# Block 1's query and index stages: a third pair of buffers, merged copies, small PSUM banks, pooled rows kept apart

## The chip, the cores and the metric

The kernel runs on one core of a Trainium2 chip. A core has five engines that run their own instruction streams and meet at semaphores: TensorE (PE, matrix products into PSUM), ScalarE (ACT), VectorE (DVE), GpSimd (POOL) and SyncE (SP, which here only issues DMAs). The metric is the device time of one execution in microseconds, as the median of several runs.

## The reference, cut to what matters

The program is two transformer blocks, one after the other, over 1024 tokens of width 1024 in float32. Only block 1 is touched. It has two layers over T = 1040 tokens (16 meta tokens and 1024 rows of x), and each layer does this:

```
proj = rms_norm(x) @ w_in            # q, k, v, gate_a, u_b, gate_b, q_idx, k_idx, w_idx, merge
q = rope(rms_norm(q per head)); k = rope(rms_norm(k)); q_idx = rope(q_idx); k_idx = rope(k_idx)
score = sum_h relu(q_idx[h] . k_idx) * w_idx[h]     # 8 index heads
attn  = softmax attention of 8 heads over the 256 best-scored visible keys of each query
y_a   = (attn * silu(gate_a)) @ w_a
pooled = windowed mean of u_b (windows 2, 4, 8, 16) minus u_b
y_b   = ((pooled @ pool_w + pool_b) * pool_s * silu(gate_b)) @ w_b
x     = x + (sigmoid(merge_a) * y_a + sigmoid(merge_b) * y_b) @ w_out
```

## The kernel before, in words

Everything is held transposed: features lie on the 128 partitions and tokens (1040, padded to TP = 1044) along the free dimension. A projection of 128 output features is a "job". `project` (L683 and around it) waits for its weights, claims a PSUM area and issues 8 chunks x 3 products x 3 pieces of 348 columns, 72 matmuls, all of them at L689. The three products per chunk come from splitting each float32 operand into a high and a low part of a faster float type. Two engines prepare the weights of every job: ACT makes the high part (`weight_hi`, L1263), POOL the low part (`weight_lo`, a subtraction at L1832). Both do so two jobs ahead, in the call `after(job)`: after a job is emptied, the weights of the job two further on are split.

The order on each engine is written out by hand, one program per engine, and semaphores join them. An engine that waits holds back all that stands behind it in its own program. PSUM: `big[0]` and `big[1]` have three banks each and are claimed in turn by `claim`, which first waits until the last user of that area has been emptied; `small2` (two banks, halves `small[0]` and `small[1]`) is free during the query stage.

The query stage of a layer treats four pairs of heads (chunks c = 0 to 3), then the index key `ki` with the 8 index weights, then key and value `kv`, then the first index query `qi`. For chunk c:

- PE projects q(c). ACT takes it out of PSUM twice (L1461 the square, L1462 the copy with the gain) into the pair of buffers `sc4[2*(c%2)]` and `sc4[2*(c%2)+1]`, then splits weights (`after`).
- PE makes the mean of the squares (`head_square`) and the rotated copy (`rotated`), both by `plain` (L701).
- DVE adds epsilon (`variance`, L2169), which also empties the `head_square` area. ACT does the reciprocal root in three steps with two table loads (`root`, L1376 to L1380).
- POOL multiplies by the cosine (`times_cos`, L1859). DVE multiplies the rotated copy by the sine (L2180), adds (L2457), finishes the root (L2173, L2174) and multiplies (L2461): the chunk is `roped`.
- ACT writes the high parts of the two heads into QS (`split_q`, L1446, two instructions). DVE subtracts to get the low parts (`stack_q`, L2188, two instructions, `q_stacked`). Only after them comes DVE's `variance` of the next chunk.

On PE the order is project q(c), `head_square` and `rotated` of chunk c-1, project q(c+1). On ACT it is, for each c: take q(c) out, `root` of c-1, `split_q` of c-1. Because chunk c+2 uses the buffers of chunk c, taking it out waits for `q_stacked` of chunk c.

The index stage (`index_stage`, L1008 scores, L999 rotations) has four chunks of 14 score units. PE alternates between `big[1]` and `small2` for the units; ACT applies relu (L1538), DVE multiplies and adds into SC (L2506, L2509). In between, PE projects the next job, chunk by chunk, into `big[0]`. ACT takes that next job out (`take_qi`, L1501, or `gate_a`, L1508, a Silu) before it applies the first relu of a chunk.

The pool stage has four groups g. PE: project u(g), `pool_mixed` of g-1, project gateb(g). ACT copies u(g) to `tm[0]` once `pool_mixed` of g-1 has been done (L1560), then scales (L1552). POOL computes the windowed mean in `tm[1]` and `tm[2]` and the difference into `tm[0]` (L1935 to L1946). DVE runs the top-256 search meanwhile.

## Time and profile before

| what | value |
|---|---|
| median of 3 runs | 3425.78 us (3425.72 to 3428.19) |
| the profiled execution | 3429.99 us, of which the span is 3428.2 us |
| PE busy | 3239.9 us (95%) |
| DVE / ACT / POOL busy | 1697.1 / 1213.8 / 1179.7 us |
| mean granted TensorE clock | 0.978 |
| HBM traffic | 175.31 MB read, 52.16 MB written |

The span runs from the first to the last instruction. Layer 0's query stage lies at about 65 to 170 us, its index stage at 170 to 267 us, its pool stage at 267 to 372 us; layer 1's stand about 906 us later. In a timeline a row that says "x48" merges that many instructions; what stands in square brackets is the idle time of the engine before the row, and what ended it.

### The profile page before, as it was taken

What the parts mean: (1) busy time and instruction counts of PE and PEld (TensorE: products, weight loads), DVE (VectorE), ACT (ScalarE), POOL (GpSimd) and SP (SyncE); (2) the same over time, 40 slices, a digit from 0 to 9 for tenths busy, and PEclk for the clock granted to TensorE, in tenths of its full rate; (3) what the DMA queues carried; (4) which work ended last, traced back from release to release, by engine and by line L of the source; (5) the groups of instructions that cost most, each with busy time, mean ns of one, the idle gap of its engine ahead of it and who ended that gap; (6) DMA issues with size and microseconds to landing.
All of it is one profiled execution on the core that took longest, in us unless ns stands there. A gap on an engine that the chain in (4) does not pass through costs nothing.

```text
span 3428.2 us, 41994 instructions
## 1 busy us (share of the span) xinstructions
PE 3239.9 (95%) x16770; PEld 2763.4 (81%) x16770; DVE 1697.1 (50%) x2682; ACT 1213.8 (35%) x1842; POOL 1179.7 (34%) x843
## 2 busy tenths in 40 slices
PE   6989999998998999999998999999998999999997
PEld 6779999998977778789775788878786688888885
DVE  6579998453256799965435044344435221000014
ACT  5552221452265422125414245345423412222222
POOL 3326532115233283321343342321543423333332
PEclk9999999999999999999999999999999999999998
DMA  5111223214311112220131411111332111111111
GB/s 155 31 32 32 66 78 97 50 26 150 119 57 31 31 44 78 90 85 17 67 133 37 168 53 36 48 50 41 135 127 68 43 50 50 44 49 50 43 50 56
DMA packets 292151, 228.41 MB, mean 67 GB/s; under 512 B 37351, under 2 KB 266390, under 8 KB 291574
## 3 DMA queue, kind: packets, MB, share of 16 engines
q1 hardware_dynamic: 264278, 122.38, 13.2%
q0 software_dynamic: 21920, 82.13, 6.4%
q10 hardware_dynamic: 5760, 21.22, 1.5%
q8 instruction: 134, 2.20, 0.3%
q14 instruction: 59, 0.48, 0.0%
HBM read 175.31 MB, written 52.16 MB: 66 GB/s over the span
## 4 chain that ended last, share of the span: by engine, by line
PE 72%; POOL 8%; issue 7%; DVE 7%; ACT 4%; DMA 2%; ACTq 0%; POOLq 0%; DVEq 0%
PE big L689 55%; PE small L838 4%; PE big L801 2%; POOL wsp L1832 2%; PE small L752 2%; PE big L817 2%; PE small L689 1%; POOL tm L1935 1%; PE big L741 1%; PE big L723 1%; DVE X L2613 1%; DMA tm<-gate_b_scratch 1%; PE small L932 1%; POOL H L1832 1%; DVE tm L2387 1%
## 5 line engine op out<-in xcount | busy, mean ns | idle before, releaser
L689 PE MATMUL big<-H,wsp 128*128 128x512 f32 (+3 forms) x9024 | 1892.3, 369 | 65.3 <-POOL H L1832 29.4
L689 PEld LDWEIGHTS big<-H,wsp 128*128 128x128 f32 (+1 forms) x9024 | 1600.3, 190 | 321.9 <-POOL H L1832 34.4
L1832 POOL TENSOR_TENSOR wsp<-raw,wsp 128x1024 fp32r<-128x1024 f32 (+2 forms) x246 | 542.8, 2207 | 1472.3 <-ACT wsp L1263 1461.5
L689 PE MATMUL big<-SP,wsp 128*128 128x512 f32 x1920 | 452.3, 396 | 0.0
L689 PEld LDWEIGHTS big<-SP,wsp 128*128 128x128 f32 x1920 | 360.5, 188 | 89.9 <-issue 0.7
L1263 ACT ACTIVATE wsp<-raw 128x1024 fp32r<-128x1024 f32 (+2 forms) x246 | 238.0, 968 | 502.4 <-PE big L689 374.0
L2543 DVE MAX8 top<-SC 128x8 f32<-128x528 f32 (+4 forms) x320 | 360.3, 1126 | 0.0
L2547 DVE MATCH_REPLACE8 SC<-top,SC 128x528 f32<-128x528 f32 (+4 forms) x320 | 358.0, 1121 | 0.0
L2701 DVE TENSOR_TENSOR X<-X,big 128x1024 f32<-128x1024 f32 (+1 forms) x26 | 29.6, 1138 | 478.4 <-PE big L689 478.4
L838 PE MATMUL small<-V,PT_a 128*128 128x64 f32 x1152 | 146.2, 272 | 0.1
L838 PEld LDWEIGHTS small<-V,PT_a 128*128 128x128 f32 x1152 | 141.3, 191 | 3.7 <-ACT PT_a L1360 0.4
L1311 ACT ACTIVATE rows_a<-rows_a,head_min 128x1040 f32<-128x1040 f32 (+7 forms) x129 | 101.4, 786 | 119.2 <-DVE head_min L2277 119.1
L2509 DVE SCALAR_TENSOR_TENSOR SC<-tm,widx,SC 128x1040 f32<-128x1040 f32 (+6 forms) x98 | 97.2, 1016 | 54.5 <-ACT tm L1538 53.3
L1983 POOL COPY meta_p<-rows_a 128x16 f32<-128x16 f32 x128 | 25.2, 197 | 262.0 <-ACT rows_a L1311 262.0
L1786 ACT ACTIVATE tm<-big,b_ff 128x1024 f32<-128x1024 f32 x32 | 35.7, 1116 | 223.2 <-PE big L689 223.2
L2277 DVE CUSTOM_DVE_ANT_0 rows_a<-big,SC 128x16 f32<-128x16 f32 (+6 forms) x112 | 77.1, 688 | 73.8 <-PE big L805 60.9
L1832 POOL TENSOR_TENSOR H<-tm,H 128x1044 fp32r<-128x1044 f32 (+3 forms) x40 | 85.3, 2137 | 79.3 <-ACT H L1386 79.3
L801 PE MATMUL big<-KK,QS 128*128 128x512 f32 (+4 forms) x416 | 105.1, 363 | 1.3 <-DVE head_min L2277 1.3
L689 PE MATMUL big<-QS,wsp 128*128 128x348 f32 (+1 forms) x480 | 95.5, 361 | 8.2 <-POOL QS L1832 4.2
L1832 POOL TENSOR_TENSOR SP<-tm,SP 128x1024 fp32r<-128x1024 f32 x40 | 96.6, 2414 | 18.0 <-ACT SP L1386 18.0
L689 PEld LDWEIGHTS big<-QS,wsp 128*128 128x128 f32 x480 | 85.1, 196 | 18.6 <-issue 10.1
L752 PEld LDWEIGHTS small<-V,PT_b 128*128 128x128 f32 x704 | 93.7, 191 | 6.2 <-ACT V L1697 4.1
(324 smaller groups left out, 3676.6 us busy)
## 6 DMA issues: line engine op xcount, KB each, us to landing
raw<-in_w_in SPq DMA_DIRECT2D x108, 512.0 KB, 3.8
raw<-in_w_ff SPq DMA_DIRECT2D x64, 512.0 KB, 4.1
raw<-in_w_out SPq DMA_DIRECT2D x24, 512.0 KB, 5.1
gate_b_scratch<-tm POOLq DMA_DIRECT2D x16, 522.0 KB, 3.0
gate_a_scratch<-tm ACTq DMA_DIRECT2D x16, 522.0 KB, 2.9
tm<-gate_a_scratch POOLq DMA_DIRECT2D x16, 522.0 KB, 3.8
tm<-gate_b_scratch POOLq DMA_DIRECT2D x16, 522.0 KB, 4.6
tm<-xT_scratch POOLq DMA_DIRECT2D x16, 522.0 KB, 5.1
```

What stands on the lines that cost most here:

```text
L689: mm = pe.matmul(dst(o, width), w[wp][:, k, 0:cols], rhs(xp, k)[:, t0:t0 + width], start=(k == 0 and i == 0), stop=(k == rows - 1 and i == 2))
L752: mm = pe.matmul(small[slot_b(u)][:, at:at + HD], PT_b[0:rows, k % 2, kt, :], v, start=(opens_b(u) and i == 0), stop=(closes_b(u) and i == ...
L801: mm = pe.matmul(big[0][:, o:o + w], u["q"], KK[:, part, o:o + w], start=(part == 0), stop=(part == 1))
L817: mm = pe.transpose(big[1][:, at:at + P], rows_a[:, k % 2, META + kt * P:META + (kt + 1) * P], ident[:])
L838: mm = pe.matmul(out[:, u["h"] * HD:(u["h"] + 1) * HD], PT_a[:, k % 2, kt, :], V[:, kt, :], start=(u["h"] == 0 and kt == 0), stop=False, s ...
L1263: act.activation(view(wsp[:, n % 2, 0, :]), view(raw[:, n % RAW, :]), ACT.Copy)\
L1311: act.activation(row, row, ACT.Exp, bias=least, scale=-1.0, accum_out=total).then_inc(*S.inc("exped", *key))
L1832: pool.tensor_tensor(dst, src, hi.bitcast(F32), ALU.subtract).then_inc(*S.inc(name, *key))
L2277: return dve.tensor_tensor_reduce(out=row, in0=logits, in1=mask, scale=-SCALE, scalar=start, op0=ALU.add, op1=ALU.min, accum_out=out)
L2509: ins = dve.scalar_tensor_tensor(sc, r, w, sc, ALU.mult, ALU.add)
L2543: dve.max(top8[:, j, :], searched[j]).then_inc(*S.inc("eight", l, r, j))
L2547: dve.match_replace(searched[j], top8[:, j, :], searched[j], TAKEN).then_inc(*S.inc("taken", l, r, j))
```

## The change

- **Three pairs in turn.** `q_pair(c)` gives chunk 1 the second pair, chunk 2 a third pair laid over X, chunks 0 and 3 the first pair. Chunk 2 now waits only for X's last readers, chunk 3 for `q_stacked` of chunk 0, `kv` for that of chunk 1.
- **ACT's order in the query stage.** It was: take q(c), root(c-1), split(c-1). It is: take q(0), take q(1), root(0), and then in turn take the next job, split the chunk two before it, root of the chunk one before it.
- **Whole copies.** `ki` and its 8 index weights leave PSUM by one ACTIVATE of 72 partitions instead of two. Key and value leave by one of 128 partitions instead of two of 64 (the gain is 1.0 for the value rows, set by a memset, and a constant load less).
- **Small banks.** The turned index weights and turned values go to `small[1]` and `small[0]` and claim no large area; PE's order around `kv` moves `rotated` of k behind the values' transposes, and the last of these waits for `w_ready`.
- **Index stage.** The next job is taken out after the first relu of a chunk, its weights are split before the third. The first gate is copied (Copy) there, and its Silu follows in place after the stage.
- **Pool stage.** The difference stays in the window buffer, `tm[1 + g%2]`, so that u(g) is copied once `pooled` of g-1 is done. Some slots and waits of later gates change with it.

```diff
+        def q_pair(c):
+            return (sc4[0], sc4[1]) if c in (0, 3) else (sc4[2], sc4[3]) if c == 1 else (q_third[:, 0, :], q_third[:, 1, :])
+        k4 = [sc4[i] for i in (2, 3, 0, 1)]
...
# ACT, query stage
-                for c in range(5):
-                    if c < 4:
-                        s, x, y = psum_of[("q", l, c)], sc4[2 * (c % 2)], sc4[2 * (c % 2) + 1]
-                        act.wait_ge(*S.at("projected", ("q", l, c)))
-                        if c >= 2:
-                            act.wait_ge(*S.at("q_stacked", "q", l, c - 2))
...
-                    if c >= 1:
-                        root(("head", "q", l, c - 1))
-                        split_q("q", (l, c - 1), sc4[2 * ((c - 1) % 2)], QS, 2 * (c - 1))
+                take_q(0)
+                take_q(1)
+                root(("head", "q", l, 0))
+                for c, take in enumerate((lambda: take_q(2), lambda: take_q(3), take_ki, take_kv)):
+                    take()
+                    split_queries(c)
+                    if c < 3:
+                        root(("head", "q", l, c + 1))
...
+                    act.activation(v3(tm[0:HD + 8, 3, :]), ps3(psum_of[("ki", l)], slice(0, HD + 8)), ACT.Copy)\
+                        .then_inc(*S.inc("raw_copied", "ki", l))
...
+                    act.activation(v3(k4[1]), ps3(s), ACT.Copy, scale=qk_gain[:, l, 1:2])\
+                        .then_inc(*S.inc("raw_copied", "k", l))
# ACT, index stage
-                    if c < 3:
-                        take_qi(c + 1)
-                    else:
-                        gate_a(0, 3, ("roped", "qi", l, 3))
                     for at, (hh, j) in enumerate(index_order(c)):
+                        if at == 1:
+                            if c < 3:
+                                take_qi(c + 1)
+                            else:
...
+                                act.activation(v_of(l, tm[:, 3, :]), ps_of(l, psum_of[("gatea", l, 0)]), ACT.Copy)\
+                                    .then_inc(*S.inc("gate_kept", "gatea", l))
+                        elif at == 2:
+                            after(("qi", l, c + 1) if c < 3 else ("gatea", l, 0))
# ACT, pool stage
-                    act.wait_ge(*S.at("score_added", l, *score_units[-1]) if g == 0 else S.at("pool_mixed", l, g - 1))
+                    act.wait_ge(*S.at("score_added", l, *score_units[-1]) if g == 0 else S.at("pooled", l, g - 1))
# PE
-                s = claim(("w", l), [("w_ready", l)])
-                pe.wait_ge(*S.at("w_copied", l))
...
-                head_norm_and_rotate(("k", l), sc4[1][0:HD], HD, sc4[0][0:HD])
-                s = claim(("v", l), [("v_ready", l)])
-                pe.wait_ge(*S.at("v_copied", l))
+                plain("head_square", ("k", l), headmean[0:HD, 0:HD], [k4[0][0:HD]], pieces1, ...)
+                pe.wait_ge(*S.at("raw_copied", "k", l))
                 for kt in range(NQ):
+                    pe.transpose(small[0][:, kt * HD:(kt + 1) * HD], k4[1][HD:P, META + kt * P:META + (kt + 1) * P],
...
+                pe.wait_ge(*S.at("w_ready", l))
+                pe.transpose(small[1][:, 0:HD], meta_v8[HD:P], ident[HD:P, HD:P]).then_inc(*S.inc("v_turned", l))
+                plain("rotated", ("k", l), rot1[0:HD, 0:HD], [k4[1][0:HD]], pieces1, ...)
# POOL
-                    pool.tensor_tensor(tm[:, 0, :], src, tm[:, 0, :], ALU.subtract).then_inc(*S.inc("pooled", l, g))
+                    pool.tensor_tensor(src, src, tm[:, 0, :], ALU.subtract).then_inc(*S.inc("pooled", l, g))
```

## Rows read from the trace of the kernel before

**Rows 1.** The page, chain that ended last, share of the span by engine.

```profile
PE 72%; POOL 8%; issue 7%; DVE 7%; ACT 4%; DMA 2%; ACTq 0%; POOLq 0%; DVEq 0%
```

**Rows 2.** Timeline of PE, query stage, layer 0 (last row: layer 1).

```profile
81.05 1.92 PE L701 MATMUL big<-SC,headmean 128*128 128x348 f32 x6
86.12 3.67 PE L701 MATMUL big<-SC,rot 128*128 128x348 f32 x6 [3.15 <-ACT SC L1462]
89.25 11.97 PE L689 MATMUL big<-H,wsp 128*128 128x348 f32 x72
...
140.08 11.88 PE L689 MATMUL big<-H,wsp 128*128 128x448 f32 x48 [0.98 <-DVE tm L2180]
...
160.37 10.02 PE L689 MATMUL big<-H,wsp 128*128 128x448 f32 x48 [1.66 <-ACT V L1520]
...
992.58 2.48 PE L701 MATMUL big<-SC,rot 128*128 128x348 f32 x6 [3.14 <-ACT SC L1462]
```

**Rows 3.** Timeline of ACT, query stage, layer 0.

```profile
80.16 2.17 ACT L1446 ACTIVATE QS<-SC 64x1044 fp32r<-64x1044 f32 x2 [5.62 <-DVE SC L2461]
83.87 1.04 ACT L1461 ACTIVATE SC<-big 128x1044 f32<-128x1044 f32 x1 [1.54 <-DVE QS L2188]
...
85.96 0.67 ACT L1263 ACTIVATE wsp<-raw 128x576 fp32r<-128x576 f32 x1
...
132.53 2.17 ACT L1446 ACTIVATE QS<-SC 64x1044 fp32r<-64x1044 f32 x2 [5.50 <-DVE SC L2461]
```

**Rows 4.** Timeline of DVE, query stage, layer 0.

```profile
81.27 2.51 DVE L2188 TENSOR_TENSOR QS<-SC,QS 64x1044 fp32r<-64x1044 f32 x2 [1.14 <-ACT QS L1446]
83.70 1.23 DVE L2169 TENSOR_SCALAR tm<-big 128x1044 f32<-128x1044 f32 x1
...
140.06 2.69 DVE L2465 TENSOR_TENSOR tm<-tm 64x1044 f32<-64x1044 f32 x1
144.99 2.51 DVE L2194 TENSOR_TENSOR KK<-tm,KK 64x1044 fp32r<-64x1044 f32 x2 [2.24 <-ACT KK L1453]
153.90 1.24 DVE L2169 TENSOR_SCALAR tm<-big 64x1044 f32<-64x1044 f32 x1 [6.40 <-PE big L701]
...
159.84 1.24 DVE L2173 SCALAR_TENSOR_TENSOR tm<-tm 64x1044 f32<-64x1044 f32 x1 [0.41 <-ACT tm L1380]
...
167.04 2.20 DVE L2188 TENSOR_TENSOR QIPB<-qi_first,QIPB 64x896 fp32r<-64x896 f32 x2 [1.02 <-ACT QIPB L1446]
```

**Rows 5.** Timeline of POOL, the same stage.

```profile
139.29 2.35 POOL L1832 TENSOR_TENSOR wsp<-raw,wsp 128x1024 fp32r<-128x1024 f32 x1 [0.61 <-ACT wsp L1263]
141.61 3.42 POOL L1859 TENSOR_TENSOR SC<-SC,trig 64x1044 f32<-64x1044 f32 x1
```

**Rows 6.** Line L2188: one group, duration in ns as min/median/max.

```profile
L2188 DVE TENSOR_TENSOR Q<-tm,Q x16: 1218/1221/2587, 1994.5 to 2410.1; 64x1024 fp32r<-64x1024 f32 x16
```

**Rows 7.** Busy time by stretch: PE, PEld, DVE, ACT, POOL, then the granted clock.

```profile
86.00:89.00 3.00, 2.88 (x5) 1.85 (x6) 0.00 (x0) 2.97 (x4) 2.29 (x2) 0.51 0.03 5
```

**Rows 8.** Timeline of PE, index stage, layer 0.

```profile
196.37 0.99 PE L1008 MATMUL small<-KK,QIPB 128*128 128x512 f32 x4 [1.41 <-ACT tm L1538]
...
219.60 1.77 PE L999 MATMUL big<-tm,rot 128*128 128x448 f32 x4 [1.59 <-ACT tm L1538]
...
246.30 1.53 PE L1008 MATMUL small<-KK,QIPB 128*128 128x512 f32 x4 [3.08 <-ACT tm L1538]
247.63 2.63 PE L689 MATMUL big<-H,wsp 128*128 128x348 f32 x9
```

**Rows 9.** Timeline of PE, pool stage, layer 0 (last row: layer 1).

```profile
293.50 23.13 PE L689 MATMUL big<-H,wsp 128*128 128x348 f32 x144 [1.19 <-ACT tm L1560]
...
370.30 1.99 PE L701 MATMUL big<-tm,pw 128*128 128x348 f32 x6 [1.52 <-POOL tm L1946]
...
1276.14 2.67 PE L701 MATMUL big<-tm,pw 128*128 128x348 f32 x6 [2.25 <-POOL tm L1946]
```

**Rows 10.** Timeline of DVE, start of the attention, layer 0.

```profile
618.64 0.17 DVE L2277 CUSTOM_DVE_ANT_0 rows_a<-big,SC 128x16 f32<-128x16 f32 x1 [28.76 <-PE big L805]
```

More of the change, by code:

```diff
@@ L584, in _ @@
             for half in range(2):
-                for which, name in enumerate(("q_norm_gain", "k_norm_gain")):
+                for which, name in enumerate(("q_norm_gain", "k_norm_gain")[0:2 - half]):
                     consts.append((qk_gain[half * HD:(half + 1) * HD, :, which], a[name].rearrange("l d -> d l")))
@@ L1476, in _ @@
-                s = psum_of[("kv", l)]
-                act.wait_ge(*S.at("projected", ("kv", l)))
-                act.wait_ge(*S.at("q_stacked", "q", l, 2))
-                act.activation(v3(sc4[0][lo64]), ps3(s, lo64), ACT.Square).then_inc(*S.inc("head_squared", "k", l))
-                act.activation(v3(sc4[1][lo64]), ps3(s, lo64), ACT.Copy, scale=qk_gain[lo64, l, 1:2])\
-                    .then_inc(*S.inc("raw_copied", "k", l))
-                act.activation(meta_v8[HD:P].rearrange("p (h q) -> p h q", h=HEADS),
-                               big[s][HD:P, 0:META].unsqueeze(1).broadcast_to([HD, HEADS, META]), ACT.Copy)\
-                    .then_inc(*S.inc("meta_v_copied", l))
@@ L1485, in _, with take_q @@
-                act.activation(v3(sc4[1][HD:P]), ps3(s, slice(HD, P)), ACT.Copy).then_inc(*S.inc("v_copied", l))
-                after(("kv", l))
+                lo64 = slice(0, HD)
+                def take_q(c):
+                    s, (x, y) = psum_of[("q", l, c)], q_pair(c)
+                    act.wait_ge(*S.at("projected", ("q", l, c)))
+                    if c == 2:
+                        act.wait_ge(*S.at("normed", "rms", l, 1, KC - 1))
+                        act.wait_ge(*(S.at("x_saved", l - 1, 7) if l else S.at("x_stored")))
+                    elif c == 3:
+                        act.wait_ge(*S.at("q_stacked", "q", l, 0))
+                    act.activation(v3(x), ps3(s), ACT.Square).then_inc(*S.inc("head_squared", "q", l, c))
+                    act.activation(v3(y), ps3(s), ACT.Copy, scale=qk_gain[:, l, 0:1])\
+                        .then_inc(*S.inc("raw_copied", "q", l, c))
+                    after(("q", l, c))
@@ new lines, in take_ki, with take_kv @@
+                def take_ki():
+                    act.wait_ge(*S.at("projected", ("ki", l)))
+                    act.activation(v3(tm[0:HD + 8, 3, :]), ps3(psum_of[("ki", l)], slice(0, HD + 8)), ACT.Copy)\
+                        .then_inc(*S.inc("raw_copied", "ki", l))
+                    after(("ki", l))
+                def take_kv():
+                    s = psum_of[("kv", l)]
+                    act.wait_ge(*S.at("projected", ("kv", l)))
+                    act.wait_ge(*S.at("q_stacked", "q", l, 1))
+                    act.activation(v3(k4[0][lo64]), ps3(s, lo64), ACT.Square).then_inc(*S.inc("head_squared", "k", l))
+                    act.activation(meta_v8[HD:P].rearrange("p (h q) -> p h q", h=HEADS),
+                                   big[s][HD:P, 0:META].unsqueeze(1).broadcast_to([HD, HEADS, META]), ACT.Copy)\
+                        .then_inc(*S.inc("meta_v_copied", l))
+                    act.activation(v3(k4[1]), ps3(s), ACT.Copy, scale=qk_gain[:, l, 1:2])\
+                        .then_inc(*S.inc("raw_copied", "k", l))
+                    after(("kv", l))
@@ L1489, in _ @@
                 act.activation(widx[:, 1:NQ, :],
-                               big[psum_of[("w", l)]][:, 8:NQ * 8].rearrange("p (j h) -> p j h", h=8), ACT.Copy,
+                               small[1][:, 8:NQ * 8].rearrange("p (j h) -> p j h", h=8), ACT.Copy,
                                scale=IDX_SCALE).then_inc(*S.inc("w_ready", l))
@@ L1502, in take_qi @@
                         .then_inc(*S.inc("raw_copied", "qi", l, c))
-                    after(("qi", l, c))
                 def gate_a(c, slot, wait):
+                    if c == 0:
+                        act.activation(v_of(l, tm[:, slot, :]), v_of(l, tm[:, slot, :]), ACT.Silu)\
+                            .then_inc(*S.inc("gatea_silu", l, c))
+                        act.wait_ge(*S.at("gatea_silu", l, c))
+                        act.dma_start(sg_d[c], tm[:, slot, :]).then_inc(*S.dma(f"gate_out{c % 2}", "a", l, c))
+                        return
                     act.wait_ge(*S.at("projected", ("gatea", l, c)))
@@ L1514, in _ @@
                 take_qi(0)
+                after(("qi", l, 0))
                 root(("head", "k", l), lo64)
-                s = psum_of[("v", l)]
                 act.wait_ge(*S.at("v_turned", l))
-                act.activation(V[:, 0:8, :], big[s][:, 0:8 * HD].rearrange("p (k d) -> p k d", k=8), ACT.Copy)\
+                act.activation(V[:, 0:8, :], small[0].rearrange("p (k d) -> p k d", k=8), ACT.Copy)\
                     .then_inc(*S.inc("v_part", l))
-                act.activation(V[:, 8, :], big[s][:, 8 * HD:9 * HD], ACT.Copy).then_inc(*S.inc("v_ready", l))
+                act.activation(V[:, 8, :], small[1][:, 0:HD], ACT.Copy).then_inc(*S.inc("v_ready", l))
                 nrelu = 0
@@ L2452, in _ @@
                 for c in range(4):
[L2453 removed]
+                    x, y = q_pair(c)
                     def rotate_q():
```

63 lines of the change are left out of this document (29 added, 34 removed).

## The prediction

> **What bounds the kernel now.** I read the chain of waits first: PE holds 72% of it, POOL only 8% [rows 1]. The busy share of PE (95% of the span) agrees. So what counts is where PE waits in the three stages that the change touches, and I went through PE's timeline there and then through those of the engines that release it. The reader is to see three things in them. In the query stage PE waits 3.15 us for a copy on ACT, in both layers, and the granted clock is then 0.51 for some three microseconds, the lower of the two levels (1.2 GHz) [rows 2, 7]. In the index stage it waits for relus that stand behind ACT's take-out of the next job [rows 8]. In the pool stage it waits 1.19 us for the copy of u, three times a layer, and once for the pooled rows [rows 9]. Behind these stages PE runs dense products until the attention. There DVE had been idle for 28.76 us when PE's first logits came, so its top-256 search is not what is late [rows 10]. What PE gains or loses here goes to the end one for one, in each of two layers (the second repeats the first 906.46 us later, by its rotation [rows 2]).
>
> **Query stage, the new order on ACT.** The third pair lets q(2) be taken out without waiting for chunk 0's stacking. But the edit also places `split_q` of chunk c behind the take-out of chunk c+2, so behind that projection. DVE's order is not changed: stack(c), then variance(c+1), and variance(c+1) empties the PSUM area that the projection of the job c+3 (q(3), ki, kv) claims. That closes a loop: projection, take-out, weight split, split_q, stack_q, variance, next projection. Before, split(0) began at 80.16, while q(2) was still being projected; so stack and variance were off PE's path. I walk the new loop in layer 0.
>
> Its terms: a projection 11.9 us. Take-out 2.1 us (from 83.87 to 85.96) and the weight split 0.67 us for ki, 1.1 us otherwise [rows 3]. The first stack instruction starts 1.1 us after split_q, and the two take 1.25 us each, then variance 1.23 us [rows 3, 4].
>
> There is a second cost in it. DVE's instruction at 140.06 took 2.69 us: POOL's subtraction ran from 139.29 to 141.64, DVE ended 1.1 us after that, and POOL's next instruction took 3.42 us instead of some 2.4, as if it had waited 1.1 us in turn [rows 4, 5]. The stack instruction itself, the same helper line in block 2, shows 1.22 us at the median and 2.59 us at most [rows 6]. So I read that a DVE instruction with two SBUF inputs and a POOL instruction pass one after the other, by turns. Before, POOL's two instructions of a chunk (weight_lo, times_cos) ran while DVE was idle. Now they are released by the same take-out and weight split that release split_q, and lie exactly on the two stack instructions. The Trainium skill (SBUF — State Buffer, Who interferes with whom) has this as a rule: a DVE instruction with two SBUF inputs contends with a GpSimd instruction that reads SBUF, and the one that starts first holds the shared port pair for the whole instruction. By that rule the stacks wait; without it the sum below would be 18.4 us lower, and the trace's 2.69 us speaks for it.
>
> - q(2) ends at 81.2 (its last matmul meets the row at 81.05). Take-out and split of ki's weights to 84.0; split_q's first half to 85.1. POOL has ki's weight_lo (1.3 us, by its 576 columns) until 85.4, DVE 1.1 to 86.5, POOL's times_cos 2.4 to 88.9, DVE 1.1 to 90.0, variance to 91.3. q(3) starts at 91.4 (before: 89.25 [rows 2]).
> - q(3) ends at 91.4 + 11.9 + 1.9 (the clock, below) = 105.2; split_q at 108.4; weight_lo to 110.8, DVE 111.9, times_cos 114.3, DVE 115.4, variance 116.7: ki starts.
> - ki ends at 130.5; its take-out is now one copy of 1.0 us, so split_q at 132.6; 135.0, 136.1, 138.5, 139.6, variance 140.9: kv starts.
> - kv ends at 154.7. Square 1.0, meta rows 0.3, one whole copy 1.1, weights 1.1: split_q of chunk 3 at 158.2.
> - From split_q(3) on nothing is reordered on DVE: before it was 132.53, and the split of ki ended at 147.50, 15.0 us later: 173.2. Variance of k, which then waited for PE until 153.90, now follows at once: 174.4. From there 4.7 us to the first step after the root (155.14 to 159.84) and 9.4 us to the end of the first index stack (159.84 to 169.24) [rows 3, 4]: 188.5.
>
> The index stage began at 170.4 (160.37 + 10.02 [rows 2]). The loss is 18.2 us a layer, 36.4 in both.
>
> **The clock in it.** PE now stands idle before q(3), ki and kv for 5.9, 7.2 and 7.3 us. After 3.15 us of idling, six matmuls took 3.67 us instead of 2.0; the projection at 140.08 took 11.88 us for 48 matmuls where the one at 160.37 took 10.02 [rows 2, 7, 9]. I take 1.9 us for each of the three gaps. Bounds: 0, and 3.8 (twice, since these gaps are twice as long).
>
> **What the other edits of this stage are worth.** The merged copies are in the walk (1.0 us each). The small banks and the moved rotation take away claims and waits around w, v and k; PE now arrives there before the chain ki split, variance k, root, qi is through, so they are covered by it and worth nothing; without that cover it would be the 0.98 and 1.66 us of idling that PE shows there and one clock loss of 1.9 us. The third pair's own waits (X stored) ended long before. The constant load less and a small memset lie in the start-up: nothing, at most 0.6 us either way.
>
> **Index stage.** The relu before the take-out frees small2 at once: PE's wait of 1.41 us in chunk 1 goes. In chunk 2 the rotation needs relu and copy both; only the weight split of 1.1 us leaves the way and the relu no longer overlaps PE's scores: 0.6 of the 1.59 us (bounds 0 and 1.59); in chunk 0 nothing. In chunk 3 the Silu with its table load, its DMA and the weight split leave: 3.08 us, and the slow clock behind it, 0.5 us (1.53 against 0.99) and 1.2 us (2.63 against 9 x 0.161) [rows 8, 9]. Together 6.8 us a layer, 13.6 in both. What is late next is the relu of the third unit behind the weights, covered by a projection chunk of PE. The Silu is done in place ahead of u's copy; it delays weight_lo for u(1) by some 3 us, and PE's gateb(0), 11.6 us of dense products, covers it (without that, 3 us).
>
> **Pool stage.** u(g) is copied at the end of its projection, not after the 2.0 us of mixing. PE's wait of 1.19 us goes for g = 1, 2, 3; POOL's chain starts 1.9 us earlier, and with it the pooled rows for which PE waits at the end (1.52 us; 2.25 us in layer 1). So 1.2 + 1.2 + 1.9 = 4.3 us in layer 0, and in layer 1 the same and 0.7 us of slow clock (2.67 against 1.99) [rows 9]: 9.3 in both.
>
> **Sum.** 36.4 - 13.6 - 9.3 = +13.5 us. On the profiled execution's 3429.99 us that is 3443.5. That execution lies 4.2 us above the median of the runs, 3425.78, so I predict 3439.3, in round numbers 3439 us.
>
> **Rivals.**
> 1. The stacks don't wait for POOL (DVE works on beside it): 2.35 + 3.4 + 3.4 = 9.2 us a layer less, 18.4 in both. Time 3420.9: not slower. Its place is DVE's two stack instructions; it decides the sign once less than a quarter of the computed port waiting comes. For it: POOL's records are rough, and the median stack in block 2 is short [rows 6]. Against it: the three long durations in rows 4 to 6.
> 2. The port wait comes, but the clock doesn't fall in the new gaps: 3 x 1.9 x 2 = 11.4 less, 3427.9, no change to be measured. Against it stand both layers' 3.15 us gaps.
> 3. Neither comes: 3409.5, faster; the gains of the two later stages are then nearly all that is left.
> 4. The longer gaps cost 3.8 us of clock each: 11.4 more, 3450.7.
> 5. The take-out wins and the change does what it says: q(2) starts its rotation 2.6 us earlier (83.5 for 86.12). It is true in the walk too, but the area of the next projection is not free by then, so PE only moves its idle time from before the rotation to behind it.
>
> **Chances.** Forecast 0.55 (its own range 3431 to 3448), rival 1 0.20, rival 2 0.10, rival 3 0.05, rival 4 0.10; rival 5 is no case of its own, its gain is in the walk. The range that holds 8 in 10 takes in rival 1 and rival 4: 3419 to 3450. About 0.2%, 6.9 us, is what a measurement can tell from no change. Slower by more: forecast and rival 4 less a tail of 0.03, 0.62. Faster by more: rival 3 and a third of rival 1, 0.12. Within: 0.26.
>
> **What would show it.** In the profile after: ACT's split_q of chunk 0 starts behind the take-out of q(2), near 84; PE idles 5 us and more before q(3), ki and kv, released by DVE's variance (L2169), with a granted clock near 0.5 behind it; DVE's stack instructions (L2188 on QS) take 2.3 us or more at the median for chunks 1 to 3's loops instead of 1.24; the index stage starts near 188 us. In the index stage the idle time before the third unit of chunk 3 is gone, in the pool stage the three waits of 1.19 us. The prediction is wrong if the stacks stay at 1.24 us (rival 1), if PE waits less than 2 us before ki and kv (the loop is not what I say), or if the time is below 3432.

## The result and the profile after

The changed kernel takes 3440.85 us (median of 5 runs, 3435.77 to 3441.11) against 3425.78 us before (3423.26 to 3428.19): ratio 1.0039, 95% interval 1.0027 to 1.0051. It is slower, by 0.4%. The prediction was 3439 us.

| what | before | after |
|---|---|---|
| median | 3425.78 us | 3440.85 us |
| the profiled execution, its span | 3429.99, 3428.2 us | 3440.85, 3439.0 us |
| mean granted TensorE clock | 0.978 | 0.973 |
| PE busy | 3239.9 us | 3247.9 us |

The end of a stage is read from PE's timeline, by the start of its first instruction of a kind. "Query" runs from the first `head_square` to the first index score, "index" to the last index score, "pool" to the start of the last `pool_mixed`. What lies outside these stages differs by 0.4 us between the two traces.

| us, layer 0 / layer 1 | before | after | difference |
|---|---|---|---|
| query | 104.79 / 105.43 | 121.34 / 119.55 | +16.55 / +14.12 |
| index | 96.29 / 96.07 | 91.47 / 90.83 | -4.82 / -5.24 |
| pool | 103.78 / 102.74 | 99.07 / 98.06 | -4.71 / -4.68 |

So the two later stages do what the change is for, and the query stage loses more than both gain. In layer 1 a little of the pool stage's gain is lost again behind this mark, in the last `pool_mixed` itself (below). Lines stand some 9 to 36 further down in this kernel: `project` is now L698, `plain` L710, ACT's take-outs L1473, L1474, L1480 and L1492, `split_q` L1454, DVE's `variance` L2203, `stack_q` L2222, POOL's `weight_lo` L1866 and `times_cos` L1893.

The timeline of PE in the query stage of layer 0 (start, duration, line, what, count, idle time before and what ended it), answering to [rows 2]:

```profile
83.58 2.02 PE L710 MATMUL big<-SC,rot 128*128 128x348 f32 x6 [0.40 <-ACT q_third L1474]
91.23 14.17 PE L698 MATMUL big<-H,wsp 128*128 128x348 f32 x72 [5.63 <-DVE tm L2203]
...
116.54 13.47 PE L698 MATMUL big<-H,wsp 128*72 128x348 f32 x72 [6.96 <-DVE tm L2203]
...
140.11 13.68 PE L698 MATMUL big<-H,wsp 128*128 128x348 f32 x72 [6.59 <-DVE tm L2203]
...
172.89 3.35 PE L710 MATMUL big<-qi_first,rot 128*128 128x448 f32 x4 [0.62 <-DVE tm L2203]
```

The rotation of q(1) no longer waits 3.15 us for the copy, only 0.40. But the projections of q(3), ki and kv each wait for DVE's variance, which empties their PSUM area, and each then takes 13.5 to 14.2 us instead of 11.9. The same stretch on ACT, DVE and POOL shows why variance is late, answering to [rows 3 to 5]:

```profile
81.47 1.04 ACT L1473 ACTIVATE q_third<-big 128x1044 f32<-128x1044 f32 x1 [6.71 <-PE big L698]
82.40 1.12 ACT L1474 ACTIVATE q_third<-big,qk_gain 128x1044 f32<-128x1044 f32 x1
83.41 0.68 ACT L1271 ACTIVATE wsp<-raw 128x576 fp32r<-128x576 f32 x1
83.99 2.16 ACT L1454 ACTIVATE QS<-SC 64x1044 fp32r<-64x1044 f32 x2
```

```profile
85.08 4.94 DVE L2222 TENSOR_TENSOR QS<-SC,QS 64x1044 fp32r<-64x1044 f32 x2 [4.58 <-ACT QS L1454]
89.95 1.23 DVE L2203 TENSOR_SCALAR tm<-big 128x1044 f32<-128x1044 f32 x1
...
109.44 5.89 DVE L2222 TENSOR_TENSOR QS<-SC,QS 64x1044 fp32r<-64x1044 f32 x2 [9.75 <-ACT QS L1454]
...
158.25 2.51 DVE L2222 TENSOR_TENSOR QS<-SC,QS 64x1044 fp32r<-64x1044 f32 x2 [9.69 <-ACT QS L1454]
```

```profile
84.17 1.40 POOL L1866 TENSOR_TENSOR wsp<-raw,wsp 128x576 fp32r<-128x576 f32 x1 [10.14 <-ACT wsp L1271]
85.54 3.38 POOL L1893 TENSOR_TENSOR SC<-SC,trig 128x1044 f32<-128x1044 f32 x1
108.53 2.35 POOL L1866 TENSOR_TENSOR wsp<-raw,wsp 128x1024 fp32r<-128x1024 f32 x1 [19.60 <-ACT wsp L1271]
110.84 3.39 POOL L1893 TENSOR_TENSOR q_third<-q_third,trig 128x1044 f32<-128x1044 f32 x1
```

ACT's split_q starts at 83.99, behind take-out and weight split. DVE's two stack instructions, 2.51 us alone (158.25, with POOL idle), take 4.94 and 5.89 us beside POOL's two. POOL's times_cos is held in turn: 3.38 us instead of some 2.4. It ends at 88.92, and DVE's pair 1.1 us behind it, at 90.02, as if DVE's second instruction had started only then.

Busy time by stretch (PE, PEld, DVE, ACT, POOL, then the granted clock, the DMA share and GB/s), at the start of the three late projections, answering to [rows 7]:

```profile
91.30:95.00 3.70, 3.70 (x13) 3.70 (x14) 2.40 (x2) 3.64 (x4) 0.00 (x0) 0.50 0.02 4
116.60:120.00 3.40, 3.40 (x12) 2.84 (x13) 2.41 (x2) 3.35 (x3) 0.00 (x0) 0.50 0.00 0
140.20:144.00 3.80, 3.80 (x13) 3.80 (x14) 2.38 (x2) 3.74 (x4) 0.00 (x0) 0.50 0.00 0
```

PE is busy all the time there and has the lower level, 1.2 of 2.4 GHz, behind each of these three gaps.

In the index stage (PE, layer 0), answering to [rows 8], the waits of 1.41 and 3.08 us are gone and the 1.59 us in chunk 2 are 1.09, but a new wait of 1.32 us stands in chunk 1. The 0.44 us in chunk 3 are not new: they stood at the same place before (PE at 241.11). Below PE's rows, DVE and POOL in chunk 1:

```profile
220.19 1.33 PE L1017 MATMUL big<-KK,QIPB 128*128 128x512 f32 x6 [1.32 <-DVE tm L2214]
...
236.50 1.74 PE L1008 MATMUL big<-tm,rot 128*128 128x448 f32 x4 [1.09 <-ACT tm L1523]
...
257.50 1.05 PE L1017 MATMUL small<-KK,QIPB 128*128 128x512 f32 x4 [0.44 <-ACT tm L1571]
```

```profile
213.52 5.61 DVE L2545 SCALAR_TENSOR_TENSOR SC<-tm,widx,SC 128x1040 f32<-128x1040 f32 x2 [0.57 <-ACT tm L1571]
219.05 1.08 DVE L2214 TENSOR_TENSOR tm<-big,trig 128x896 f32<-128x896 f32 x1
```

```profile
212.63 2.30 POOL L1893 TENSOR_TENSOR tm<-tm,trig 128x896 f32<-128x896 f32 x1 [17.50 <-ACT tm L1523]
214.88 3.42 POOL L1866 TENSOR_TENSOR wsp<-raw,wsp 128x1024 fp32r<-128x1024 f32 x1
```

In the pool stage (PE, one row of layer 0 and one of layer 1), answering to [rows 9], the three waits of 1.19 us for the copy of u are gone; the wait for the last pooled rows stays, shorter. In layer 1 the mixing behind it is slower than before (3.47 us instead of 2.67), since more of it runs at the lower clock:

```profile
377.54 1.99 PE L710 MATMUL big<-tm,pw 128*128 128x348 f32 x6 [1.19 <-POOL tm L1980]
...
1287.59 3.47 PE L710 MATMUL big<-tm,pw 128*128 128x348 f32 x6 [1.89 <-POOL tm L1980]
```

### The profile page after: what moved, and what is told of

The parts are those of the page before. It is cut to its first block, busy times and chain, and to the rows that moved or that the text cites. A ratio compares the mean times of both kernels' runs of the same rounds, so it can differ in the third digit from the quotient of the medians.

```text
span 3439.0 us, 41988 instructions
## 1 busy us (share of the span) xinstructions
PE 3247.9 (94%) x16770; PEld 2769.4 (81%) x16770; DVE 1711.5 (50%) x2683; ACT 1209.7 (35%) x1840; POOL 1185.6 (34%) x843
## 4 chain that ended last, share of the span: by engine, by line
PE 76%; DVE 7%; POOL 6%; issue 5%; ACT 4%; DMA 2%; ACTq 0%; POOLq 0%; DVEq 0%
PE big L698 58%; PE small L847 4%; PE big L810 2%; PE small L761 2%; PE big L826 2%; POOL wsp L1866 1%; PE small L698 1%; POOL tm L1969 1%; PE big L750 1%; PE big L732 1%; DVE X L2649 1%; DVE QS L2222 1%; PE small L1017 1%; PE small L941 1%; DMA tm<-gate_b_scratch 1%
## 5 line engine op out<-in xcount | busy, mean ns | idle before, releaser
L698 PE MATMUL big<-H,wsp 128*128 128x512 f32 (+3 forms) x9024 | 1899.9, 370 | 88.1 <-DVE tm L2203 38.4
L698 PEld LDWEIGHTS big<-H,wsp 128*128 128x128 f32 (+1 forms) x9024 | 1606.5, 191 | 345.2 <-DVE tm L2203 41.7
L1866 POOL TENSOR_TENSOR wsp<-raw,wsp 128x1024 fp32r<-128x1024 f32 (+2 forms) x246 | 542.4, 2205 | 1448.7 <-ACT wsp L1271 1437.8
L698 PE MATMUL big<-SP,wsp 128*128 128x512 f32 x1920 | 452.0, 395 | 0.0
L698 PEld LDWEIGHTS big<-SP,wsp 128*128 128x128 f32 x1920 | 360.2, 188 | 89.8 <-issue 0.7
L2579 DVE MAX8 top<-SC 128x8 f32<-128x528 f32 (+4 forms) x320 | 306.9, 959 | 0.0
L2583 DVE MATCH_REPLACE8 SC<-top,SC 128x528 f32<-128x528 f32 (+4 forms) x320 | 304.2, 951 | 0.0
L1866 POOL TENSOR_TENSOR H<-tm,H 128x1044 fp32r<-128x1044 f32 (+3 forms) x40 | 85.3, 2137 | 80.6 <-ACT H L1394 80.6
L698 PE MATMUL big<-QS,wsp 128*128 128x348 f32 (+1 forms) x480 | 96.3, 363 | 8.1 <-POOL QS L1866 4.2
L1866 POOL TENSOR_TENSOR SP<-tm,SP 128x1024 fp32r<-128x1024 f32 x40 | 96.5, 2413 | 18.0 <-ACT SP L1394 18.0
L698 PEld LDWEIGHTS big<-QS,wsp 128*128 128x128 f32 x480 | 85.6, 197 | 18.8 <-issue 10.1
```

The costliest lines, as they stand in the source:

```text
L698: mm = pe.matmul(dst(o, width), w[wp][:, k, 0:cols], rhs(xp, k)[:, t0:t0 + width], start=(k == 0 and i == 0), stop=(k == rows - 1 and i == 2))
L1866: pool.tensor_tensor(dst, src, hi.bitcast(F32), ALU.subtract).then_inc(*S.inc(name, *key))
L2579: dve.max(top8[:, j, :], searched[j]).then_inc(*S.inc("eight", l, r, j))
L2583: dve.match_replace(searched[j], top8[:, j, :], searched[j], TAKEN).then_inc(*S.inc("taken", l, r, j))
```

## The experiments

Every experiment was timed 4 to 12 times beside the kernel before on the same chip; ratios are to that kernel, and for the changed kernel the ratio is 1.0039. Executions of one kernel differ by up to 13 us (the kernel before on one chip: 3419.22 to 3431.64 us), in part in places that no edit here touches: with split_q first the stretch ahead of the first `head_square` took 62.17, 62.73 and 65.94 us in three traces, and what follows layer 1's pool stage 2146.64, 2145.02 and 2148.05 us. The stages are steadier: in these three traces each repeats within 0.5 us. In layer 0's query stage that is partly luck: each of the three traces has one fall of the granted clock there, two of them in front of or in qi(0), one at the rotation of q(1), and a fourth trace of the same order ("weights later") has none and took 94.88 us. So 1.5 to 2 us of chance lie in layer 0's query stage. Layer 1 has no such fall in any of the four: 94.89, 94.94, 94.89 and 94.89 us. The stage times decide where a few microseconds matter, and the medians say whether the whole moved. No run undoes the edits of the index and the pool stage: what they gain is read from these stages, which are nearly the same in every kernel that has the edits (the last row of the table has one more), and it isn't split among them.

| us, layer 0 / layer 1 | query | index | pool |
|---|---|---|---|
| changed kernel | 121.34 / 119.55 | 91.47 / 90.83 | 99.07 / 98.06 |
| split_q first | 96.38 / 94.89 | 91.43 / 90.81 | 99.07 / 98.06 |
| POOL behind the stack | 111.81 / 108.74 | 91.45 / 90.78 | 99.07 / 98.07 |
| PE kept busy | 114.69 / 114.56 | 91.33 / 90.85 | 99.08 / 98.07 |
| two pairs, split_q first | 99.34 / 98.21 | 91.44 / 90.81 | 99.07 / 98.07 |
| split_q first, again | 96.88 / 94.94 | 91.42 / 90.80 | 99.07 / 98.07 |
| large banks, split_q first | 103.40 / 100.06 | 91.32 / 90.75 | 99.06 / 98.05 |
| separate copies, split_q first | 98.42 / 98.64 | 91.13 / 90.83 | 99.07 / 98.06 |
| weights later, split_q first | 94.88 / 94.89 | 91.44 / 90.84 | 99.07 / 98.06 |
| POOL behind the score, split_q first | 96.46 / 94.97 | 90.68 / 90.06 | 99.06 / 98.06 |

### Split_q ahead of the take

```diff
                 for c, take in enumerate((lambda: take_q(2), lambda: take_q(3), take_ki, take_kv)):
-                    take()
                     split_queries(c)
+                    take()
```

> The changed kernel with one edit: on ACT, split_q of chunk c stands before the take-out of the next job again, all else as changed. Theory (the order closes a loop over split_q, stack_q and variance, and puts the stacks under POOL's instructions): PE's idle times of 5.6, 7.0 and 6.6 us before q(3), ki and kv go, the three slow-clock stretches behind them too, the stacks on QS return to 2.5 us a pair. The query stage ends some 3 us earlier than in the kernel before, the gains of index and pool stage (10.1 and 9.0 us) stay: 3425.8 - 19.0 - 6 = 3401 us, between 3395 and 3408. Rival (the new buffers or merged copies themselves cost the time): no change, 3435 to 3441.

Measured: 3384.22 us (3381.11 to 3390.25), ratio 0.9883 (0.9868 to 0.9898). A second and a third time, on another chip: 3388.68 us, 0.9891 (0.9877 to 0.9905), and 3388.5 us, 0.9885 (0.9868 to 0.9901). The query stage falls by 24.96 and 24.66 us and is then 8.4 and 10.5 us shorter than before the change. PE, DVE and POOL there:

```profile
81.20 2.02 PE L710 MATMUL big<-SC,rot 128*128 128x348 f32 x6 [1.50 <-ACT q_third L1474]
82.80 11.86 PE L698 MATMUL big<-H,wsp 128*128 128x348 f32 x72
...
98.54 11.84 PE L698 MATMUL big<-H,wsp 128*72 128x348 f32 x72
...
114.10 11.86 PE L698 MATMUL big<-H,wsp 128*128 128x348 f32 x72
...
129.64 11.55 PE L698 MATMUL big<-H,wsp 128*128 128x448 f32 x48 [1.26 <-ACT SC L1492]
```

```profile
77.86 2.51 DVE L2222 TENSOR_TENSOR QS<-SC,QS 64x1044 fp32r<-64x1044 f32 x2 [1.14 <-ACT QS L1454]
80.30 1.23 DVE L2203 TENSOR_SCALAR tm<-big 128x1044 f32<-128x1044 f32 x1
```

```profile
81.80 1.40 POOL L1866 TENSOR_TENSOR wsp<-raw,wsp 128x576 fp32r<-128x576 f32 x1 [11.55 <-ACT wsp L1271]
```

The three projections start without a wait and take 11.86, 11.84 and 11.86 us. The stacks take 2.51 us; POOL begins only when they are over. One swap of two calls carries the whole loss of the query stage. It was faster than expected (3395 to 3408 us), which said that other edits of the stage are worth something once the loop is gone; the runs below test that.

### The port: POOL held until DVE has stacked

```diff
                 for c in range(5):
+                    if c >= 2:
+                        pool.wait_ge(*S.at("q_stacked", "q", l, c - 2))
                     after(("q", l, c) if c < 4 else ("ki", l))
```

> The changed kernel with one added wait: POOL splits weights and multiplies by the cosine for a chunk only when DVE's stacks of the chunk before have been done; ACT's order stays as changed. Theory (port by turns): the three stack pairs fall from 4.9, 5.9, 5.9 us to 2.5 us, PE's idle times before q(3), ki, kv shrink by 2.4, 3.4 and 3.4 us, 18.2 us in both layers: 3440.9 - 18.2 = 3422.7 us, between 3419 and 3427. Rival (the stacks are slow for another reason, or POOL's lateness is passed on to the root and rotation): 3438 to 3448.

Measured: 3415.71 us (3412.08 to 3421.65), ratio 0.9974 (0.9966 to 0.9983). The query stage falls by 9.53 and 10.81 us. DVE, POOL and PE, layer 0 (PE's last row: layer 1):

```profile
81.72 2.51 DVE L2224 TENSOR_TENSOR QS<-SC,QS 64x1044 fp32r<-64x1044 f32 x2 [4.73 <-ACT QS L1454]
84.15 1.23 DVE L2205 TENSOR_SCALAR tm<-big 128x1044 f32<-128x1044 f32 x1
```

```profile
84.31 1.40 POOL L1866 TENSOR_TENSOR wsp<-raw,wsp 128x576 fp32r<-128x576 f32 x1 [13.79 <-DVE QS L2224]
85.67 2.42 POOL L1893 TENSOR_TENSOR SC<-SC,trig 128x1044 f32<-128x1044 f32 x1
```

```profile
85.44 14.50 PE L698 MATMUL big<-H,wsp 128*128 128x348 f32 x72 [3.20 <-DVE tm L2205]
...
107.69 13.19 PE L698 MATMUL big<-H,wsp 128*72 128x348 f32 x72 [3.58 <-DVE tm L2205]
...
990.91 11.71 PE L698 MATMUL big<-H,wsp 128*128 128x348 f32 x72 [3.21 <-DVE tm L2205]
```

With no more than a wait added on POOL, the stacks are back at 2.51 us, times_cos at 2.42 us, and PE's waits shrink from 5.63, 6.96 and 6.59 to 3.20, 3.58 and (at kv) 3.22 us: 9.18 us a layer, where the prediction's port term was 9.2. Rival 1 of the prediction is out. Five of the six projections stay slow (14.50, 13.19 and 13.26 us in layer 0, 12.93 and 13.25 us in layer 1), so a gap of 3.2 us can cost the clock as much as one of 5.6. It doesn't always: q(3) in layer 1 waited 3.21 us and took 11.71 us, and the granted clock stayed at 1.00 there. This is why the time came out below the expected 3419 to 3427 us: the query stage fell by 20.3 us in both layers, 18.3 of it waits.

### The clock: PE kept busy in its gaps

```diff
+                def keep_busy(count):
+                    for i in range(count):
+                        pe.matmul(small2[:, 0:PIECE1], rot1[:], trig1[:, 0, 0:PIECE1], start=True, stop=True)
+                pe.wait_ge(*S.at("rotary_tables", l))
...
+                    if c >= 3:
+                        keep_busy(7 if c == 3 else 9)
...
+                keep_busy(8)
                 project(("kv", l), hi_lo(H), pieces1, [("raw_copied", "k", l)])
```

> The changed kernel with 7, 9 and 8 extra products on PE into small2, whose result nobody reads, before the projections of q(3), ki and kv, where PE idles. Theory (the clock falls because PE idles): the projections behind take 11.9 us again instead of 14.2, 13.5, 13.7 (layer 0) and 13.2, 13.0, 13.4 (layer 1), 9.7 us in all, if the extra products end before the idle time does: 3440.9 - 9.7 = 3431.2 us, between 3428 and 3434. Rival (the slow stretches come from something else, such as the power of the whole core): 3439 us or more.

Measured: 3425.08 us (3422.05 to 3431.45), ratio 1.0001 (0.9992 to 1.0011). PE, layer 0:

```profile
83.36 4.26 PE L1053 MATMUL small<-trig,rot 128*128 128x348 f32 x14
89.17 11.70 PE L698 MATMUL big<-H,wsp 128*128 128x348 f32 x72 [1.55 <-DVE tm L2211]
```

Busy time by stretch from the first added products to the end of kv, as above:

```profile
83.00:146.00 63.00, 57.42 (x292) 46.76 (x291) 38.83 (x24) 28.00 (x26) 15.29 (x6) 1.00 0.10 26
```

The added products change no result and release nobody; each shows as two matmuls, so the 7 are x14. The granted clock is 1.00 through all three gaps. The three projections take 11.70, 11.63 and 11.71 us, in layer 1 11.71, 11.64 and 11.70, and the query stage falls by 6.65 and 4.99 us, 11.6 in both; the prediction's clock term was 11.4. Rival 2 is out as well. The time lies below the expected 3428 to 3434 us, and 4 us more came off the median than off the query stage. The added wait for the rotary tables costs 0.89 us of PE's time in layer 1 and the stretch between the layers grew by 5.4 us, which is the edit's own cost or a disturbance and not settled.

### The third pair alone

The kernel with split_q first, and the third pair taken away: q(2) uses chunk 0's buffers and q(3) chunk 1's, each waiting for `q_stacked` as before the change. Key and value then use chunk 2's buffers and wait for its stack, which costs nothing: PE waits 1.26 us before qi(0) as with split_q first.

```diff
-            return (sc4[0], sc4[1]) if c in (0, 3) else (sc4[2], sc4[3]) if c == 1 else (q_third[:, 0, :], q_third[:, 1, :])
+            return (sc4[2 * (c % 2)], sc4[2 * (c % 2) + 1])
...
```

> As the run with split_q first, and without the third pair of buffers: two pairs in turn, so that q(2) is taken out after the stacks of chunk 0, as in the kernel before. Theory: this brings back the idle time of 3.15 us before the rotation of chunk 1 and its slow clock, 1.5 us + 1.8 us a layer against the run with three pairs: some 6 us more, 3407 us if that one takes 3401. Rival (the third pair is worth nothing once split_q stands first, the chain of stacks decides anyway): the same time within 2 us.

Measured: 3394.2 us (3392.38 to 3395.57), ratio 0.991 (0.9896 to 0.9924), 10.0 us above split_q first on the same chip. The query stage is 2.96 and 3.32 us longer, 6.3 for the pair, as expected. The rest is not explained by the edit: between the two traces it lies in the stretch between the layers and behind layer 1's pool stage, which differ from run to run. The take-out of q(2) waits again for the stack, and the rotation of q(1) behind it:

```profile
82.53 3.41 PE L710 MATMUL big<-SC,rot 128*128 128x348 f32 x6 [3.02 <-ACT SC L1471]
```

So the pair removes 1.5 of those 3.0 us and the fall of the clock behind them. It is worth 6.3 us where split_q comes first, and it needs no order in which split_q comes late.

### The small banks

Split_q first, and w's and v's turned rows in large areas again, with `rotated` of k ahead of the values (what the expectation calls keys' turned rows are these two):

```diff
-                    mm = pe.transpose(small[1][:, j * 8:(j + 1) * 8],
+                s = claim(("w", l), [("w_ready", l)])
+                    mm = pe.transpose(big[s][:, j * 8:(j + 1) * 8],
...
-                    pe.transpose(small[0][:, kt * HD:(kt + 1) * HD],
+                s = claim(("v", l), [("v_ready", l)])
+                    pe.transpose(big[s][:, kt * HD:(kt + 1) * HD],
...
```

> Split_q first, and one part of the change undone: keys' turned rows take the large banks again instead of small ones, in the order of the kernel before. Theory (the small banks are worth something as soon as the projections no longer wait at the pair): the projection that comes behind waits for keys' turned rows to be taken out, some 2.8 us a layer as in the trace of before, and the clock falls once more, some 1.9 us: 2 x 4.7 = 9, so 3392 us (3389 to 3396). Rival (the bank is free in time anyway): as split_q first alone, 3384 us.

> The changed kernel with split_q ahead of the take, a second time, as the base of the three kernels beside it. It took 3384.2 us (0.9883 of the kernel before) the first time; both theories expect 3384 again (3380 to 3390), ratio 0.988.

Measured: 3398.2 us (3394.71 to 3401.82), ratio 0.9922 (0.9908 to 0.9935), 9.5 us above its base of the same chip, 3388.68 (3382.47 to 3390.65). The 9 us were expected; the time lies above 3389 to 3396 us because the base is higher than the 3384 us it was reckoned from. The query stage is 6.52 and 5.12 us longer. PE, layer 0:

```profile
132.49 0.60 PE L1064 MATMUL big<-ident,tm 8*128 8x8 f32 x7 [1.80 <-ACT SC L1493]
135.29 12.30 PE L698 MATMUL big<-H,wsp 128*128 128x448 f32 x48 [2.21 <-DVE tm L2215]
...
152.57 1.77 PE L710 MATMUL big<-qi_first,rot 128*128 128x448 f32 x4 [0.63 <-DVE SC L2215]
156.01 10.04 PE L698 MATMUL big<-H,wsp 128*128 128x448 f32 x48 [1.66 <-ACT V L1548]
```

Four waits for an emptied area stand where the base has one (1.28 us). The banks, with the order of `rotated`, are worth 11.6 us by the stages.

No run takes the small banks out of the changed kernel itself, so what they are worth there is not shown. The trace after speaks against "nothing". With large areas, qi(0) claims the area that DVE's sine product of ki empties (the 2.21 us above; 0.98 us in [rows 2]). In the changed kernel PE and DVE show:

```profile
156.37 10.03 PE L698 MATMUL big<-H,wsp 128*128 128x448 f32 x48 [0.15 <-ACT SC L1492]
```

```profile
163.46 1.24 DVE L2214 TENSOR_TENSOR tm<-big,trig 64x1044 f32<-64x1044 f32 x1 [2.69 <-POOL tm L1893]
```

The product ended at 164.70, so with large areas qi(0) would have started 8.3 us later than it did, and PE has waits of only 1.6 us between qi(0) and the first index score to take that up. An estimate from these rows is a loss of 5 us or more a layer.

### The whole copies

Split_q first, and two ACTIVATEs each in place of the whole copies of ki with its weights and of key with value:

```diff
...
-                    act.activation(v3(k4[1]), ps3(s), ACT.Copy, scale=qk_gain[:, l, 1:2])\
+                    act.activation(v3(k4[1][lo64]), ps3(s, lo64), ACT.Copy, scale=qk_gain[lo64, l, 1:2])\
                         .then_inc(*S.inc("raw_copied", "k", l))
+                    act.activation(v3(k4[1][HD:P]), ps3(s, slice(HD, P)), ACT.Copy).then_inc(*S.inc("v_copied", l))
```

> Split_q first, and one part of the change undone: two copies again in place of each whole copy of keys and values. Theory: each extra copy costs its fixed part on the engine that takes the bank out, and little of it reaches PE: about 1 us a layer, so 3386 us (3384 to 3390). Rival 1: nothing reaches PE, 3384 us. Rival 2: the bank is late for the next projection and the clock falls with it, 3 us a layer or more, so 3390 us.

Measured: 3391.46 us (3390.83 to 3393.82), ratio 0.9903 (0.989 to 0.9917), 2.8 us above the base; the intervals overlap. It lies just above the expected 3384 to 3390 us. The query stage is 1.54 and 3.70 us longer. PE's waits for the two copies are 1.42 us instead of 0.37 and 2.33 us instead of 1.28, so one copy is 1.05 us each time, as the theory has it, and the rest is slow clock (11.46 us for the 48 matmuls behind the gap of 2.33 us, 10.04 in the base). Layer 0's 1.54 us is too small, because the base's trace has a slow stretch there that this one lacks. Its rows, with the granted clock at 0.50 from 83 to 86 us:

```profile
82.13 3.21 PE L710 MATMUL big<-SC,rot 128*128 128x348 f32 x6 [1.86 <-ACT q_third L1474]
84.62 12.61 PE L698 MATMUL big<-H,wsp 128*128 128x348 f32 x72
```

With separate copies the same two took 2.02 and 11.87 us, behind a wait of 1.51 us. From the `head_square` before to the next one that is 18.72 us in the base and 16.73 here, so 2.0 us are chance and the copies cost 3.5 us in layer 0, as in layer 1 (3.7). That is rival 2, 3 us a layer or more, and not the theory: 7.2 us in both.

The three parts measured one by one, 6.3, 11.6 and 7.2 us, make 25.1 us, more than the 18.9 us by which the stage with split_q first is shorter than before the change. They don't simply add up.

### Two tests of the new wait in the index stage

First the weight split in chunk 1 was moved on ACT from ahead of its third unit to ahead of its fourth:

```diff
-                        elif at == 2:
+                        elif at == (3 if c == 1 else 2):
```

> Split_q first, and chunk 1's weight split asked for behind the third score unit of chunk 0 instead of where it stood. Theory: the wait of 1.3 us that is new in the index stage's second chunk (DVE's two score operations, 5.61 us beside POOL's weight_lo and times_cos) goes, since weight_lo no longer runs in that place: 2 x 1.3, so 3381.5 us (3380 to 3383). Rival 1: times_cos alone delays DVE as much, the wait stays and the time is 3384 us. Rival 2: weight_lo is late for chunk 1's first score and the wait moves there, 3386 us or more.

Measured: 3386.6 us (3384.45 to 3390.93), ratio 0.9889 (0.9876 to 0.9903), index stage 91.44 and 90.84 us, as without the edit. PE waits 1.29 us as before and DVE's two units take 5.60 us. The edit moved weight_lo by only 0.5 us against the stage's start (187.47 to 188.57, where the stage started 0.6 us later), so it still stood beside the second unit. This did not tell weight_lo from times_cos. The next one moves both:

```diff
                 for c in range(4):
+                    if c == 2:
+                        pool.wait_ge(*S.at("score_added", l, 1, 0, 7))
                     times_cos(("qi", l, c), qi_temps...
```

> Split_q first, and POOL waits for DVE's second score operation of chunk 1 before it multiplies chunk 2's query by the cosines, so POOL's times_cos and weight_lo no longer stand beside DVE's first two score operations (5.6 us for the two, 1.30 us for one where POOL is idle). Theory (the new wait of 1.3 us in the second chunk is DVE held by POOL): DVE's two take some 2.6 us, the wait goes, the index stage falls from 91.4 us to 90.1 and the time by 2 x 1.3 = 2.6 us, so 3383.5 us against the 3386 us of the two results of split_q first (3380 to 3388). Rival: the two engines meet one instruction later, on the rotation, and the stage stays at 91.4 us or grows.

> The changed kernel with split_q ahead of the take, a third time, as the base of the kernel beside it: 3384 to 3389 us, index stage 91.4 us.

Measured: 3387.61 us (3380.5 to 3393.41), ratio 0.9891 (0.9874 to 0.9907); its base 3388.5 (3381.41 to 3390.94), 0.9885. The medians don't tell them apart. The index stage fell from 91.45 to 90.68 and from 90.81 to 90.06 us. DVE, then POOL:

```profile
185.45 1.30 DVE L2547 SCALAR_TENSOR_TENSOR SC<-tm,widx,SC 128x1040 f32<-128x1040 f32 x1 [0.57 <-ACT tm L1571]
187.25 2.54 DVE L2547 SCALAR_TENSOR_TENSOR SC<-tm,widx,SC 128x784 f32<-128x784 f32 x1 [0.49 <-ACT tm L1571]
189.71 1.08 DVE L2216 TENSOR_TENSOR tm<-big,trig 128x896 f32<-128x896 f32 x1
```

```profile
186.84 2.12 POOL L1893 TENSOR_TENSOR tm<-tm,trig 128x896 f32<-128x896 f32 x1 [19.75 <-DVE SC L2547]
```

The first unit is back at 1.30 us, the second still meets times_cos (2.54 us), and PE's wait of 1.29 us before the next unit is gone: POOL's place was its cause. Some 0.5 of the 1.3 us came back as smaller delays and 0.8 us a layer are left, so the stage ends between the theory (90.1) and the rival (91.4). That is too little for the medians.

## Why the prediction was right

The time was forecast within 2 us, and the sign and the mechanism with it. Two terms were off in opposite directions, -5.7 and +3.5 us, so part of that nearness is luck, and one step, the covered banks, is not shown. In the order of its steps:

- **Split_q behind the take-out closes a loop: right.** split_q(0) at 83.99 (walk: "near 84"), q(3) at 91.23 (91.4), ki at 116.54 (116.7), kv at 140.11 (140.9), split_q(3) at 157.16 (158.2). The rotation of q(1) started at 83.58 (rival 5: 83.5), and PE's idle time only moved behind it. Putting split_q first took the whole of it away.
- **The port turns, 9.2 us a layer: right.** Holding POOL back gave 9.18 us of PE's waits a layer. Without them the forecast would have been 3420.9 us. By the rule of the Trainium skill (SBUF — State Buffer, Who interferes with whom) the instruction that starts first keeps the shared port pair until it ends; the rows of DVE and POOL above agree (2.43 and 3.38 us more for DVE's pair).
- **The clock, 1.9 us a gap: right in size.** The three projections of layer 0 took 14.17, 13.47 and 13.68 us against 11.9, so 2.3, 1.6 and 1.8; in layer 1 13.21, 12.95 and 13.38, so 1.3, 1.1 and 1.5. That is 9.5 us by these durations; with PE kept busy the stage fell by 11.6 us, and 11.4 were forecast. None lost the 3.8 us of rival 4. A fourth slow stretch in each layer, from the rotation of qi(0) on, was not forecast (next point).
- **Query stage, 36.4 us in both layers: too high, it was 30.7.** Of the 5.7 us, layer 1 has 4.1: its clock losses were 1.8 us smaller than layer 0's, its stage before the change had been 0.6 us longer than layer 0's (105.43 for 104.79), which the walk of layer 0 alone could not see, and 1.65 us are common. These stand in layer 0 too: kv was 0.8 us early, and the chain through DVE ended at 186.95 (its stack of qi(0), 184.75 + 2.20), not at 188.5. PE's own stream ended with it: the first score began at 187.00 behind no wait, with the slow clock ahead of it (3.35 us for the four matmuls at 172.89, and 11.80 us for the projection behind them, where before it had 10.02). The walk's own numbers, 188.5 less 170.4, give 18.1 and not 18.2.
- **The banks covered and worth nothing: not shown, and probably wrong.** No run has the loop without the banks, and the rows under "The small banks" give an estimate of 5 us or more a layer for them beside the loop. It doesn't touch the forecast of the time, since the changed kernel has the small banks and the walk had no wait for them. Without the loop they are worth 11.6 us; the prediction's price without cover, 0.98 + 1.66 + 1.9 = 4.5 us a layer, was close to these 5.8.
- **The merged copies, 1.0 us each in the walk, 2.0 a layer: too low without the loop.** There they are worth 3.6 us a layer, since the longer wait brings the slow clock. Beside the loop no run tells.
- **Index stage, 13.6 us: too high, it was 10.1.** Chunk 3 gave 4.44 us (26.32 to 21.88), forecast 4.8; chunk 2 0.97, forecast 0.6. The step that failed is chunk 1: the wait of 1.41 us went as said, but the chunk grew from 23.01 to 23.46 us. What had moved behind the first relu is not only ACT's copy but also POOL's times_cos and weight_lo that it releases, and they now lie on DVE's score units: 1.32 us of waiting for DVE, and 0.71 us for the stack of chunk 2's query where it had been 0.44. Before, times_cos had run while DVE was idle, and only weight_lo stood on a score unit. The prediction applied the port to the query stage and did not ask for it here.
- **Pool stage, 9.3 us: the waits right, the clock not.** Of the 9.3 us, 8.6 were waits, and 9.4 were measured up to the start of the last mixing. The last wait shrank by 0.33 us (1.52 to 1.19), and 0.36 in layer 1. The other 0.7 us, the slow clock in layer 1's last mixing, did not go: it took 3.47 us instead of 2.67. To the end of that mixing the two stages gained 8.6 us.
- **Sum.** +13.5 forecast between the profiled executions, +10.9 measured: -5.7 (query), +3.5 (index), -0.1 (pool), -0.4 (outside). The medians differ by 15.1, because the profiled execution of before lies 4.2 us above its median and that of after on it. The forecast difference of 13.5 lies between the two, too high for the one and too low for the other, and that is luck.

## What to carry to other kernels

A buffer that lets a take-out run earlier is no reason to put the take-out first in an engine's program: what stood behind it may feed the instruction that empties PSUM for the projection after next. Follow each late instruction to the buffer that it frees, and count what its release starts on other engines. Here the same edits gave 0.4% slower or 1.1% faster by the order of two calls, and what three of the edits are worth was measured only with that order right. When several edits come together, find the one that sits on the path before judging the others.

## What the runs showed of the hardware

- Two queued instructions each on DVE (two SBUF inputs) and POOL go by turns: DVE's pair took 4.94 to 5.89 us instead of 2.51 and POOL's 3.38 instead of 2.42. A scalar_tensor_tensor with its inputs in SBUF suffers alike: 5.61 us for two units, where the first of them alone took 1.30. Starting POOL's work behind the end of DVE's pair, by one semaphore, brought both back to 2.51 and 2.42 us.
- The cost of the clock did not grow with the gap: behind gaps of 3.20, 5.63 and 6.96 us the projection took 14.50, 14.17 and 13.47 us. Nor did the gap alone decide whether the clock fell: 3.21 us cost nothing in layer 1 of one trace (11.71 us), where 3.20 us in layer 0 of the same trace gave the 14.50. A gap of 1.55 us behind added products cost nothing (11.70 us). At 1.3 us it went both ways: in front of qi(0) 1.26 us cost 1.4 (11.55 us for 48 matmuls, 10.13 for the next 48) in one trace of a kernel, and 1.28 us nothing (10.04 us) in another of the same. Added products of no use in the idle gaps won back 11.6 us.
